# A decoder kernel on one NeuronCore: row sums moved to VectorE, and memory projections begun ahead of two norms

## The reference

```
# first block, layer i = 0, 1  (mixer: mla for 0, dsa for 1)
x = layer_norm(ALPHA * x + mixer(x),                    ln_g[i, 0], ln_b[i, 0])   # ln0, ln3
y = memory_cross_attention(x, mem, w_q, w_kv, w_o)      # kv = mem @ w_kv, independent of x
x = layer_norm(ALPHA * x + y,                           ln_g[i, 1], ln_b[i, 1])   # ln1, ln4
x = layer_norm(ALPHA * x + swiglu_ffn(x, w_in, w_down), ln_g[i, 2], ln_b[i, 2])   # ln2, ln5
# second block
mod = silu(c) @ mod_w + mod_b            # c: [1, 1024], mod_w: [1024, 6144]
sh1, sc1, g1, sh2, sc2, g2 = split(mod, 6)
h = rmsnorm(x, norm1_g) * (1 + sc1) + sh1          # and so on: fox attention, pool, conv ffn
```

## Time and profile before

| | |
|---|---|
| time, median of 3 runs | 2393.86 us (2391.39 to 2396.46) |
| the profiled execution's own time | 2390.52 us |
| its span | 2388.7 us |
| mean granted TensorE clock, share of 2.4 GHz | 0.98 |
| TensorE busy | 2276.4 us, 95% of the span |
| VectorE busy | 1250.2 us, 52% |
| ScalarE busy | 1017.6 us, 43% |
| GpSimd busy | 160.9 us, 7% |
| DMA | 219.04 MB, mean 92 GB/s |

### The profile page before, as it was taken

How to read it: one execution, slowest core, us unless ns; L and a number is a source line. 1 busy time by engine, 2 the same in 40 slices (tenths; PEclk the granted TensorE clock), 3 DMA queues, 4 the chain that set the end, 5 groups by cost and what they waited for, 6 DMA issues and landing times.

```text
span 2388.7 us, 47718 instructions
## 1 busy us (share of the span) xinstructions
PE 2276.4 (95%) x18862; PEld 2150.6 (90%) x18862; DVE 1250.2 (52%) x2516; ACT 1017.6 (43%) x1576; POOL 160.9 (7%) x186
## 2 busy tenths in 40 slices
PE   7999999999999989888999999999989998999998
PEld 7978899899999978767899989999969897999997
DVE  4577534555552247899453455554144654656422
ACT  4566343433232144756353243232154545555413
POOL 1000100100000130145100100000030000000000
PEclk9999999999999999899999999999999999999999
DMA  5332241344552221100242234553312202333330
GB/s 159 75 101 89 89 152 52 89 132 132 136 152 90 88 81 54 37 19 1 71 157 73 72 106 132 135 151 109 105 45 89 76 27 63 89 104 89 105 106 36
DMA packets 303369, 219.04 MB, mean 92 GB/s; under 512 B 34378, under 2 KB 290320, under 8 KB 303248
## 3 DMA queue, kind: packets, MB, share of 16 engines
q1 hardware_dynamic: 251568, 189.30, 26.5%
q10 hardware_dynamic: 49920, 25.17, 4.1%
q0 software_dynamic: 1760, 2.88, 0.4%
HBM read 207.56 MB, written 2.10 MB: 88 GB/s over the span
## 4 chain that ended last, share of the span: by engine, by line
PE 88%; ACT 5%; DVE 4%; issue 2%; POOL 1%; DMA 0%; DVEq 0%; SPq 0%; POOLq 0%; ACTq 0%
PE bank L646 74%; PE bank L722 3%; PE bank L788 2%; PE bank L758 2%; PE bank L888 1%; PE bank L951 1%; PE bank L943 1%; DVE PB_D L1743 1%; ACT ST L1528 1%; PE bank L1161 1%; ACT XH L1195 1%; POOL BB L2261 1%; PE bank L1094 1%; ACT XT L1371 1%; ACT BI L1195 1%
## 5 line engine op out<-in xcount | busy, mean ns | idle before, releaser
L646 PE MATMUL bank<-XH,WH 128*128 128x256 f32 x3568 | 1003.8, 281 | 33.0 <-DVE XL L1858 24.3
L646 PE MATMUL bank<-XL,WH 128*128 128x256 f32 x3568 | 997.2, 279 | 0.0
L646 PE MATMUL bank<-XH,WL 128*128 128x256 f32 x3568 | 997.0, 279 | 0.0
L646 PEld LDWEIGHTS bank<-XH,WH 128*128 128x128 f32 x3568 | 679.7, 190 | 41.5 <-issue 31.7
L646 PEld LDWEIGHTS bank<-XL,WH 128*128 128x128 f32 x3568 | 676.4, 190 | 0.2 <-issue 0.2
L646 PEld LDWEIGHTS bank<-XH,WL 128*128 128x128 f32 x3568 | 676.2, 190 | 0.0
L613 DVE TENSOR_TENSOR WL<-RAW,WH 128x2048 fp32r<-128x2048 f32 x172 | 394.2, 2292 | 520.8 <-ACT WH L609 520.8
L609 ACT ACTIVATE WH<-RAW 128x2048 fp32r<-128x2048 f32 x172 | 328.7, 1911 | 438.3 <-PE bank L646 438.3
L646 PE MATMUL bank<-HH,WH 128*128 (+1 forms) x1056 | 291.7, 276 | 0.9 <-DVE HF L1938 0.9
L646 PE MATMUL bank<-HL,WH 128*128 (+1 forms) x1056 | 291.5, 276 | 0.0
L646 PE MATMUL bank<-HH,WL 128*128 (+1 forms) x1056 | 291.5, 276 | 0.0
(11 more groups left out here) (305 smaller groups left out, 3213.8 us busy)
## 6 DMA issues: line engine op xcount, KB each, us to landing
RAW<-in_ffn_w_in SPq DMA_DIRECT2D x88, 512.0 KB, 4.9
MB<-in_mod_w ACTq DMA_DIRECT2D x48, 512.0 KB, 5.1
RAW<-in_ffn_w_down SPq DMA_DIRECT2D x44, 512.0 KB, 4.0
RAW<-in_ffn_up SPq DMA_DIRECT2D x44, 512.0 KB, 4.5
RAW<-in_xa_w_kv SPq DMA_DIRECT2D x32, 512.0 KB, 4.4
RAW<-in_ffn_down SPq DMA_DIRECT2D x22, 512.0 KB, 3.9
RAW<-in_xa_w_q SPq DMA_DIRECT2D x16, 512.0 KB, 4.0
RAW<-in_xa_w_o SPq DMA_DIRECT2D x16, 512.0 KB, 4.4
```

Of the source, the lines that this page charges most:

```text
L646: mm = nc.tensor.matmul(out_ap[:, cols], l, moving, start=(start and n == 0 and k == 0), stop=(stop and n == len(parts) - 1 and k == len(o ...
```

## The change

1. `mod_sum` and `mod_column` are gone. DVE now also turns the summed `ACC` in blocks of 32 x 32 (`nc.vector.transpose` into `ACCT`) and reduces each block's rows (`tensor_reduce` into `MODP`, four numbers a partition). TensorE folds the partitions once a layer, after the down projection and its norm's sums, with four products against a 0/1 matrix `FOLD` of 32 columns, and DVE adds the bias for 24 columns at once (`mod_columns`). `ACC` is single instead of double, and `mod_load` waits for the eight products, not for the steps behind them.
2. In the stages around `ln0` and `ln3`, TensorE goes on to `xa_kv` without the norm: the mean's two products come after the first tile, and the sum of squares comes after the third unit as a single product, since POOL has added up the eight chunks of squares in `ZS`. ACT's and DVE's orders follow: ACT evacuates the first unit amid the squares and two more before `RSTD`; the normed chunks come two at a time in units 3, 4 and 5 and one in units 6 and 7 (`KV_CHUNKS`).

```diff
-                        if first and n == 4 and f < DEPTH:
-                            pe.wait_ge(mod_out, MOD_N * f + MOD_N - 2)
...
-                def mod_sum(m, par):
-
-                    pe.wait_ge(mod_step, m * 9 + 9)
-                    if not isinstance(m, int) or m >= 2:
-                        pe.wait_ge(mod_out, m - 1)
-                    nc.tensor.matmul(bank[4 + par][:, 0:1], ACC[:, par, 0, :], ONES[:, 0:1], start=True,
-                                     stop=True).then_inc(mod_mm, 1)
-                if f < DEPTH:
-                    wide_stage(f"ffn_in{f}", xpairs(), fill,
-                               behind=lambda i, j: mod_sum(i + MOD_N * f, j % 2))
-                else:
-                    wide_stage(f"ffn_in{f}", xpairs(), fill)
+                wide_stage(f"ffn_in{f}", xpairs(), fill)
                 down_stage(f)
                 if norm[0] == "l":
                     norm_sums(norm, (y_free, DC * f + DC), bank[1], bank[0])
-                    for m in (MOD_N - 2, MOD_N - 1):
-                        mod_sum(MOD_N * f + m, m % 2)
+                    pe.wait_ge(mod_step, MOD_S * MOD_N * (f + 1))
+                    pe.wait_ge(y_free, DC * f + 5)
+                    for b in range(4):
+                        mm = nc.tensor.matmul(bank[4][32 * b:32 * b + 32, 0:MOD_N], FOLD, MODP[:, :, b],
+                                              start=True, stop=True)
+                    mm.then_inc(mod_mm, 1)
...
+                nc.vector.tensor_tensor(ACC[:, 0, :], ACC[:, 0, :], ACC[:, 1, :], ALU.add).then_inc(mod_step, 1)
+                dve.wait_ge(mod_step, m * MOD_S + 9)
+                nc.vector.transpose(ACCT[:, :], ACC[:, 0, :]).then_inc(mod_step, 1)
+                dve.wait_ge(mod_step, m * MOD_S + 10)
+                nc.vector.tensor_reduce(MODP[:, bass.ds(n, 1), :], ACCT[:, :].rearrange("p (b r) -> p b r", r=32),
+                                        AXX, ALU.add).then_inc(mod_step, 1)
...
-                    act.wait_ge(mod_step, m * 9)
+                    act.wait_ge(mod_step, m * MOD_S - 3)
...
-            proj_norm("mla_o", "ln0")
-
-            def cross_attention(layer):
+
+            def cross_attention(layer, stage):
...
+                            if first == 0 and isinstance(i, int) and (i, k) == (0, 0):
+                                row_means(norm, (tile_free, TILE0[stage] + DC), bank[6])
                     return one
-                by_pairs(pe, 4, unit(0))
+                for i in range(3):
+                    unit(0)(i, i % 2)
+                pe.wait_ge(sq_summed, 8 * NORM_I[norm] + DC)
+                nc.tensor.matmul(bank[7][:, :], ONES, ZS[:, :], start=True, stop=True).then_inc(kv_var, 1)
+                unit(0)(3, 1)
                 by_pairs(pe, 4, unit(4))
...
+                pool.wait_ge(mean_ready, k + 1)
+                for c in range(1, DC):
+                    pool.wait_ge(squared, 8 * k + c + 1)
+                    if c > 1:
+                        pool.wait_ge(sq_summed, 8 * k + c)
+                    nc.gpsimd.tensor_tensor(ZS[:, :], SQ[:, 0, :] if c == 1 else ZS[:, :], SQ[:, c % 4, :],
+                                            ALU.add).then_inc(sq_summed, 2 if c == 1 else 1)
```

More of the change, by code:

```diff
@@ L87 @@
 K_SEL = 968
-K_N = 1224
-K_REP, K_ROT = 1224, 1352
-K_ALL = 1480
+K_FOLD = 1224
+K_N = 1256
+K_REP, K_ROT = 1256, 1384
+K_ALL = 1512
 def shape_constants():
@@ L177, in build_program @@
         ONES = KC[:, K_ONES:K_ONES + P]
+        FOLD = KC[:, K_FOLD:K_FOLD + 32]
         SEL = [KC[:, K_SEL + P * h:K_SEL + P * h + P] for h in range(2)]
@@ L912, in _ @@
             wide_stage("mla_o", xpairs(), "mla_o", behind=memory_turn(0))
-            proj_norm("mla_o", "ln0")
-            def cross_attention(layer):
+            def cross_attention(layer, stage):
                 pe.wait_ge(m_split, 4 * layer + 4)
                 name = f"xa_kv{layer}"
+                norm = f"ln{3 * layer}"
                 def unit(first):
@@ L1345, in proj_and_memory, with norm @@
                     after_unit(stage, i, i, TILE0[stage] + 2 * i + 2)
-            def norm(name, ready, var_bank, g_col, b_col, out_to_x, hi, src, then=None, later=False, before=None):
+            def norm(name, ready, var_bank, g_col, b_col, out_to_x, hi, src, then=None, later=False, before=None, amid=None):
                 k = NORM_I[name]
                 for c in range(DC):
+                    if c == 4 and amid is not None:
+                        amid[0]()
                     if before is not None:
@@ L1381, in norm, with ln @@
                         then()
-            def ln(idx, var_bank, hi=True, then=None, later=False):
+            def ln(idx, var_bank, hi=True, then=None, later=False, amid=None):
                 def col(what):
@@ L1386, in ln @@
                 return norm(f"ln{idx}", lambda c: (centred, 8 * idx + c + 1), var_bank, col("ln_g"), col("ln_b"), True, hi,
-                            ZB, then, later)
+                            ZB, then, later, amid=amid)
             mod_wv = A["mod_w_2"][0].rearrange("(c p) n -> p c n", p=P)
@@ L1398, in cross_attention @@
                 proj_and_memory(stage, layer)
-                shift = ln(3 * layer, bank[7], later=True)
                 name = f"xa_kv{layer}"
@@ L1413, in unit, with first_unit, next_units @@
                         after_unit(name, v, j, v * 2 + (TILE0[name] + 2))
-                        shift(v)
                     return unit
-                by_pairs(act, 4, kv(0))
-                by_pairs(act, 4, kv(4))
+                def first_unit():
+                    act.wait_ge(tile_free, TILE0[name])
+                    kv(0)(0, 0)
+                def next_units():
+                    kv(0)(1, 1)
+                    kv(0)(2, 0)
+                shift = ln(3 * layer, bank[7], later=True, amid=(first_unit, next_units))
+                for v in range(3, 8):
+                    first = v // 4 * 4
+                    kv(first)(v - first, v % 2)
+                    for c in KV_CHUNKS[v]:
+                        shift(c)
                 q = f"xa_q{layer}"
@@ L1895, in memory_lows, with first_lows @@
                                                 f32(MH[:, 2 * n:2 * n + 2, :]), ALU.subtract).then_inc(m_split, 1)
-                ln_proj(3 * layer, stage, memory_lows, low=False)
-                def kv(i, j):
-                    next_lo(dve, f"xa_kv{layer}", i, j)
-                    low(f"ln{3 * layer}", XT, i)
-                by_pairs(dve, 8, kv)
+                def first_lows():
+                    for v in range(3):
+                        next_lo(dve, f"xa_kv{layer}", v, v % 2)
+                ln_proj(3 * layer, stage, memory_lows, low=False, then=first_lows)
+                for v in range(3, 8):
+                    next_lo(dve, f"xa_kv{layer}", v, v % 2)
+                    for c in KV_CHUNKS[v]:
+                        low(f"ln{3 * layer}", XT, c)
                 by_pairs(dve, 4, lambda i, j: next_lo(dve, f"xa_q{layer}", i, j))
```

68 lines of the change are left out of this document (41 added, 27 removed).

## The result

The changed kernel takes 2368.69 us (median of 4 runs, 2360.2 to 2371.9) against 2395.16 us (median of 4) for the kernel before: ratio 0.9866, 95% interval 0.9841 to 0.9891, 26.5 us less by the medians (the ratio and its interval are an estimate of their own, not the quotient of the medians). The profiled execution of it took 2371.9 us, its span 2370.1.

What follows compares the result with a forecast made beforehand. TensorE, busy 95% of the span, was taken as the bound. Gains of 19.6 (modulation's sums), 15.0 (norms) and 1.0 (pace), less 0.5 (tight places), make 35.1 us: 2358.5 us, forecast 2354 to 2363, range 2352 to 2378.

Steps and rivals of the forecast that it cites:

- rival A: Up projections stay at 117.8 ns: 2376.8 us, one layer alone 2367.5, with slow down projections 2386.3; chance 0.23.
- Part 1's pace: Up projections without the modulation's products run at 113.3 ns a matmul, 10.88 us a unit, instead of 117.8 ns.
- The 19.6 us: Gain from removing 22 modulation products a layer from TensorE, 9.8 us a layer, at the faster pace.
- Turn and reduction: DVE's two added operations a column in the up projections: 0.3 us each, hidden in DVE's idle time.
- Rival C: Turn and reduction make DVE the bound of the up projection: slower, 2429 us if they take 4.6; chance 0.02.
- Part 2: At ln0 and ln3, TensorE runs xa_kv during the norm: gain 7.5 us a norm, 15.0 for both.
- 1.0 for the pace: Two breaks of the stream in each xa_kv may put part of it into the faster pace: 0.5 us each.
- the 1.29 us of POOL's additions: In xa_kv, POOL's seven additions of squares take 1.29 us each, from 279.4 to 289.2.
- with 2.3 us to spare: In xa_kv, POOL's sum is ready at 289.2, while TensorE asks for it at 291.5.
- the tightest place: 0.4 us: In xa_kv, DVE has unit 2's WL ready at 285.5, and TensorE needs it at 285.9.
- rival B: POOL's additions and DVE's splits hinder each other at the norms: 3 to 4.5 us a norm, 2366 us; chance 0.08.
- Rival D: ACT's or DVE's order holds up xa_kv's units: up to 15 us back, 2374 us, halfway 2366 likelier; chance 0.07.

Runs made afterwards that it cites:

- mod_only: The changed kernel with the norms' change undone, so only the modulation's sums are changed against the kernel before: median 2385.91 us, ratio 0.9956.
- after_again: The changed kernel, unedited, measured again: median 2364.12 us of 4 runs, ratio 0.9845 with one slow execution left out.
- narrow_adds: The changed kernel with five of POOL's seven additions of squares cut from 512 to 64 columns, so the sum is incomplete: 2396.81 us.
- norm_only: The changed kernel with the modulation's change undone, so only the norms are changed against the kernel before: median 2385.01 us, ratio 0.9936.
- after_third: The changed kernel, unedited, measured a third time: median 2370.41 us of 7 runs, ratio 0.9907.
- settle: The changed kernel with two unused one-column products behind each up projection's first unit and one behind its second: median 2362.58 us, ratio 0.9844.

## Why the prediction was right and where it was not

**The time.** 2358.5 was forecast and 2368.69 measured, inside the range but outside 2354 to 2363; 35 us less forecast, 26.5 measured. How near it came is partly luck: three medians of the same kernel lie from 2364 to 2370, and which of the forecast's cases a single execution shows is drawn. The profiled execution is rival A's one slow layer (2367.5, or 2372.3 with 4.8 for its down projection; it took 2371.9).

**Part 1's pace.** The step that failed is "I take the faster pace: `ffn_in2` is the same loop with nothing between its units and never leaves it, and the first unit of `ffn_in0`, ahead of the first product, is in it too." A few stretches of one execution were read as a property of the code. What the runs show is a draw in each execution: `ffn_in2` itself leaves the faster pace, in `mod_only` and in `narrow_adds`. The 19.6 us are the case in which both layers draw the faster pace: then they are there (9.8 us a layer in `mod_only`, 8.8 and 9.4 in `after_again`, down projections included). In the kernel before, the products flipped the pace behind each unit, so that half of each up projection was slow whatever the draw. The change keeps what is drawn for 350 us. A slow draw therefore takes back 9.5 us in the up projection and 4.6 in the down projection, which is rival A in a form that I had only half: I gave it 0.23 as a fact about the kernel, and it is one about each execution. Its price was right, 4.8 us for the down projection included. If one draw in three is slow (7 of the 23 stretches counted above are, 5 of the 12 in these two layers), and a slow draw costs 9.5 us more than it did before, two layers lose 6.3 us on average (an estimate from few draws).

**Turn and reduction.** 0.3 us each forecast, 0.312 and 0.286 measured; DVE waits 2.2 us a unit for TensorE, where about 2.3 were said. Rival C is out.

**Part 2.** 15.0 us less 0.5, and 1.0 for the pace, were forecast; the profiled executions give 12.9 (the change), 11.0 (`after_again`), 11.2 (`norm_only`) and 15.7 (`after_third`). They differ by the paces that these stages drew (`xa_kv` takes 49.8 us or 48.7 in the changed kernel, `dsa_o` 47.8 or 46.2): in `after_third` both `xa_kv` ended fast, in `after_again` and `norm_only` none did.

The terms that failed are the 1.29 us of POOL's additions, "with 2.3 us to spare", and "the tightest place: 0.4 us". Chained by a semaphore the additions start 1.44 us apart (277.96, 279.41, 280.85); seven such steps from 277.96 end at 288.0. Two of them meet a split and take 1.9 us longer each: 291.7, and the sum came at 291.63, where 289.2 was forecast. TensorE was there at 290.1, so without the meetings there would have been 2.1 us to spare: the wider steps were made up by an earlier start, the meetings were not. Each split lost 0.5 to 0.6 us, and the tightest place had 0.4. TensorE lost 1.6 and 0.4 us in waits, and some 0.3 in restarting the stream: 2.3 us a norm, 4.6 for both.

This is rival B, at 0.08: its place was right, its size of 3 to 4.5 us a norm too large, since the sum came 3.6 us later and the weights 0.6 where I had 5 and 2, and its chance too low. I had both slowed alike, where in truth only the one that starts second is held. That POOL's 28 additions before had equal lengths said only that they had met no split of `WL` (none overlaps one by more than 0.06 us). In `narrow_adds` no split starts within an addition any more, and the splits' extra time and both waits are gone, so this is shown and not argued. The GPSIMD Engine Reference of the Trainium skill (Key points) says that GpSimd shares its SBUF interfaces with VectorE and contends with VectorE's instructions that have two inputs in SBUF; the trace now agrees, with 1.31 to 3.17 us on the one side and 2.29 to 2.93 on the other.

**Rival D** did not come: ACT and DVE followed in every unit behind the third, and the two waits have the cause of B.

**The sum again.** 35.1, less 4.6 for the norms, less 6.3 for the draws: 24.2 us, beside 26.5 measured. Both the medians and the 6.3 carry several us of draws, so this agreement shows only that no large term is missing.

## What to carry to other kernels

Where two stretches of the same code differ in one profile, look at more executions before you put it down to a neighbouring instruction: here the median moved by 6 us between three measurements of one kernel. An instruction that is short in its own row can set what runs behind it; taking 22 products a layer out was worth 20 us in one execution (`mod_only`'s) and less than nothing in another (`narrow_adds`'s), and putting three back, near the start, made the up projections fast in every trace, though not the whole time steady. And when work is moved beside another engine's, equal durations in the old trace are evidence only if the two had met there; and it matters which of the two starts first, for the other one pays.

## What the runs showed of the hardware

- A stream of 256-column matmuls has two paces at a granted clock of 1.00, 113.3 and 117.8 ns (4%). It kept one over 3168 matmuls, from an up projection through the down projection behind it. At some places it changes without a product or a pause that shows: from `xa_kv` to `xa_q` in 21 of 28 times, with at most 0.122 us between two starts, and at the third unit of `ffn_in2` in three executions. It is drawn anew where the stream starts behind a pause (also at the kernel's last stage, behind a wait of 0.88 us in `settle`); at the start of an up projection it can be read only from where the granted clock has risen to 1.00. One plain float32 product of 1 or of 512 columns flips it; two of one column in a row end in the slower one, while two of 512 columns in a row left the other pace 24 times of 24. What in TensorE this is, why the pairs differ, and what changes it at an unbroken place and what decides the draw (30 of 42 fast behind a pause) stays open; no run here tells it.
- An addition of 128 x 512 on GpSimd and a split on VectorE with both operands in SBUF do not run together: the one that starts second is held until the first is done. An addition that starts within a split takes 3.17 us in place of 1.31 (of 64 columns 1.92 in place of 0.32) and the split keeps its time (2.29); a split that starts 0.8 us before an addition's end takes 2.93 in place of 2.29, and that addition keeps its 1.31. Additions on GpSimd that wait for each other start 1.44 us apart.
- The turn of 128 x 128 on VectorE takes 0.312 us and the reduction of 128 x 128 to four 0.286, about as long as an addition of the same size (0.29).
